# First mixer of an encoder layer: the second pass of its scores over 64 rows, the two banks of a chunk on different halves of TensorE's rows

## The chip, the cores and the metric

One core of one Trainium2 chip runs the whole program. The metric is the device time of one execution in microseconds (us). TensorE (PE) multiplies; its weight loads are told apart as PEld. DVE is the vector engine, ACT the scalar engine, POOL the third elementwise engine, SP issues the DMAs.

## What is computed

One layer on 2048 tokens of width 1024: a normalised input projection, two mixers side by side, an output projection, a squared-ReLU MLP and a gated addition, all in float32. The change concerns the first mixer alone, grouped-query attention with 8 query heads of 64 dimensions on 2 key and value heads:

```python
def block(q_blk):          # 128 queries at a time
    sc = jnp.einsum('bqkgd,bskd->bkgqs', q_blk, k, preferred_element_type=jnp.float32) * scale
    pr = jax.nn.softmax(sc, axis=-1)
    return jnp.einsum('bkgqs,bskd->bqkgd', pr.astype(v.dtype), v)
```

## The kernel before, in words

The program has four phases: the projection, the first mixer (`mixer_a_phase`), the second mixer, and the feed part with output projection, MLP and gate. The first mixer works in 32 units: 16 tiles of 128 queries by 2 key heads, each unit with its group of 4 query heads (G = 4).

**Products in parts.** Matmuls read float32r operands, which hold fewer bits than float32, so an operand is split into a high part (the rounded copy) and a low part (the rest). A head has 64 dimensions and the array 128 rows, so queries and keys are loaded with their 64 dimensions twice. ACT writes the high part of a unit's queries to all 128 rows of `qT` (`query_hi`, L842), and DVE then replaces rows 64 to 127 with the low part (`query_lo`, L897). `kT[g][0]` holds the keys' high part in both halves of the rows, `kT[g][1]` their low part in both. One matmul of `qT` with `kT[g][0]` thus gives high times high plus low times high, and a second pass with `kT[g][1]` adds high times low and low times low.

**Chunks.** A unit's scores are made in 8 chunks (NC), one head by half of the keys. A chunk is 1024 keys, two PSUM banks of 512, and `scores` (L764) issues for each bank the two passes, four matmuls of 128 rows by 512 columns in all, with the same weights. PE's last one increments `sc_done`; DVE takes the negative maximum (`maximum`, L901), ACT the exponential (`exponential`, L848), and the chunk's two banks are free for the chunk after next (`exp_done`).

**The loop.** `pe.Fori(0, NT)` covers two units a turn, and each unit has 16 steps s, one for each 128 keys. In step s PE turns the probabilities of 4 heads (L819, into one of two banks), ACT copies them to `pT[0]` (L876), DVE subtracts for the low part `pT[1]` (L930), and PE multiplies the values of step s - 2 (`values`, L777). In each even step the scores of one chunk of the next unit follow. Step 4 and step 12 also have the sum of the two parts of the output (`fold_out`, L786). Step 6 has the turning of the queries of the unit after next (`turn_queries`, L750); ACT's `query_hi` follows it in its step 7, and so does DVE's `query_lo`. PE's turn of step s waits until DVE has done step s - 2, since it writes the same bank. The order of the work on every engine is written out by hand in these steps; there is no planner. SP's queue brings the queries and stores the results, and POOL does small merges and sums of weight blocks beside it.

**Ahead of the loop** PE turns the queries of units 0 and 1 and all keys, ACT and DVE split them, and the 8 chunks of unit 0 are made. The remaining 256 chunks lie in the loop.

**Outside the mixer** one place matters for what follows: in the projection phase, L372 is a small matmul for bias rows, 33 rows by 8 columns of weights, between full matmuls of L358. It stands directly behind `pe.sem_inc(step, 1)` (L371) and has two records per instruction, since its operands are plain float32. It runs 8 times.

Of the kernel before, what the change touches and what calls it, by code (L numbers as in the profile page):

```python
# [16 lines left out]
F32R = mybir.dt.float32r  # L17
ACT = mybir.ActivationFunctionType
AXX = mybir.AxisListType.X

P = 128
D = 1024
S = 2048
HD = 64
NHA, NKV, NHB = 8, 2, 8
# [11 lines left out]
BANK = 512  # L37
# [512 lines left out]
def mixer_a_phase(nc, scr, ident, fold, heads, w_ff2):  # L550
# [8 lines left out]
    G = NHA // NKV  # L559
    NC = 2 * G  # L560
    NR = 4
    with ExitStack() as ctx:
        k = Kit(nc, ctx, "mixa")
        k_raw = k.sb("k_raw", [P, NT, NKV * 2 * HD])
        v_raw = k.sb("v_raw", [P, NT, NKV * HD])
        kT = [[k.sb(f"kT{g}{h}", [P, S], F32R) for h in range(2)] for g in range(NKV)]
        v_hl = k.sb("v_hl", [P, NT, NKV, 2 * HD], F32R)
        q_in = k.sb("q_in", [P, NHA * 2 * HD])
        qT = [k.sb(f"qT{g}", [P, G, P], F32R) for g in range(NKV)]
        prob = [k.sb(f"prob{u}", [P, G, S]) for u in range(2)]  # L570
        pT = [k.sb(f"pT{h}", [P, NR, BANK], F32R) for h in range(2)]
        oT = k.sb("oT", [P, 2, BANK])
# [11 lines left out]
        score = ctx.enter_context(nc.psum_tensor("mixa_score", [P, 4 * BANK], F32))  # L584
# [157 lines left out]
        @block.tensor  # L742
        def _(pe):
            def turn_queries(V, g, bank, first=False):

                pe.wait_ge(q_dma, (V - g) * 16 + 32)
                if not first:
                    pe.wait_ge(half_done, V * 2 - 2)
                for h in range(G):
                    mm = pe.transpose(bank[:, h * P:(h + 1) * P], q_in[:, (G * g + h) * P:(G * g + h + 1) * P], ident[:])  # L750
                mm.then_inc(qt_done, 1)

            def scores(V, g, c):

                half, h = c // G, c % G
                if c == 0:
                    pe.wait_ge(qt_lo, V + 1)
                if not (isinstance(V, int) and c < 2):
                    pe.wait_ge(exp_done, V * NC + c - 1)
                for j in range(2):  # L760
                    kc = 2 * half + j
                    at = 2 * (c % 2) + j
                    for part in range(2):
                        mm = pe.matmul(score[:, at * BANK:(at + 1) * BANK], qT[g][:, h, :],  # L764
                                       kT[g][part][:, kc * BANK:(kc + 1) * BANK], start=part == 0, stop=part == 1)
                mm.then_inc(sc_done, 1)

            def values(U, g, s):

                half = s // (NT // 2)  # L770
                pe.wait_ge(lo_done, U * NT + s + 3)
                if s == 0:
                    pe.wait_ge(half_done, U * 2 + 1)
                if s == NT // 2:
                    pe.wait_ge(qt_lo, U + 3)
                for part in range(2):
                    mm = pe.matmul(out_acc[half][:], v_hl[:, s, g, :], pT[part][:, s % NR, :],  # L777
                                   start=s % (NT // 2) == 0 and part == 0,
                                   stop=s % (NT // 2) == NT // 2 - 1 and part == 1)
                mm.then_inc(pv_done, 1)  # L780

            def fold_out(count, half):

                pe.wait_ge(o_done, count)
                for h in range(G):
                    mm = pe.matmul(out_acc[half][:, h * HD:(h + 1) * HD], oT[:, half, h * P:(h + 1) * P], fold[:],  # L786
                                   start=True, stop=True)
                mm.then_inc(fold_done, 1)

            pe.wait_ge(q_dma, 32)  # L790
            turn_queries(0, 0, out_acc[0], True)
            turn_queries(1, 1, out_acc[1], True)
            for n in range(2 * NT // 4):
                g, j0 = n % 2, 4 * (n // 2)
                if n % 4 == 0:
                    pe.wait_ge(k_in[n // 4], 32)
                if n >= 6:
                    pe.wait_ge(kt_lo, n - 5)
                for j in range(4):
                    mm = pe.transpose(turn_banks[n % 6][:, j * P:(j + 1) * P], k_raw[:, j0 + j, g * P:(g + 1) * P],  # L800
                                      ident[:])
                mm.then_inc(kt_done, 1)
            pe.wait_ge(kt_lo, 6)
            for c in range(NC):
                scores(0, 0, c)
            pe.wait_ge(kt_lo, 2 * NT // 4)
            pe.wait_ge(v_lo, 1)
            pe.wait_ge(set_done, 4)
            pe.wait_ge(qt_lo, 2)
            pe.matmul(out_acc[1][:], v_hl[:, NT - 3, 1, :], pT[0][:, 2, :], start=True, stop=False)  # L810
            with pe.Fori(0, NT) as it:
                for w in range(2):
                    U = it * 2 + w
                    for s in range(NT):
                        if s in (0, NT // 2):
                            pe.wait_ge(exp_done, U * NC + (G if s == 0 else NC))
                        pe.wait_ge(lo_done, U * NT + s + 1)
                        for h in range(G):
                            mm = pe.transpose(turned[s % 2][:, h * P:(h + 1) * P], prob[w][:, h, s * P:(s + 1) * P],  # L819
                                              ident[:])  # L820
                        mm.then_inc(t_done, 1)
                        if s < 2:
                            values(U - 1, 1 - w, s + NT - 2)
                        else:
                            values(U, w, s - 2)
                        if s % 2 == 0:
                            scores(U + 1, 1 - w, s // 2)
                        if s == 4:
                            fold_out(U * 2 + 1, 1)
                        if s == 6:  # L830
                            turn_queries(U + 2, w, out_acc[1])
                        if s == 12:
                            fold_out(U * 2 + 2, 0)
            values(2 * NT - 1, 1, NT - 2)
            values(2 * NT - 1, 1, NT - 1)
            fold_out(4 * NT + 1, 1)

        @block.scalar
        def _(act):
            def query_hi(V, g, bank):  # L840
                act.wait_ge(qt_done, V + 1)
                act.activation(qT[g][:].rearrange("p h n -> p (h n)"), bank[:], ACT.Copy).then_inc(qt_hi, 1)  # L842

            def exponential(V, par, c):
# [8 lines left out]
            def sums_out(U, half):  # L853

                act.wait_ge(pv_done, U * NT + (half + 1) * NT // 2 + 4)
                act.activation(oT[:, half, :], out_acc[half][:], ACT.Copy).then_inc(o_done, 1)

            query_hi(0, 0, out_acc[0])
            query_hi(1, 1, out_acc[1])
            for n in range(2 * NT // 4):  # L860
                act.wait_ge(kt_done, n + 1)
# [1267 lines left out]
def layer(nc, rel_bias, onehot, x, w_in, rope, ident_d, fold_d, w_ff2, w_tail, g_out, g_mlp_pre, g_ple,  # L2129
          g_attn_pre, g_q, g_k, g_attn_post, g_mlp_post, pT, out):  # L2130

    shapes = {"qA": (S, D_AB), "kA": (S, NKV * 2 * HD), "vA": (S, NKV * HD), "qB": (S, D_AB), "kB": (S, D_AB),
              "vB": (S + 2 * PAD, D_AB), "bias": (NHB, ROWS_W), "table": (NHB, P, ROWS_W),
              "wT": (D_FF // BANK, 5, P, 2 * BANK), "yA": (S + P, D_AB), "yB": (S, D_AB), "h2": (BT, D)}
    scr = {n: nc.dram_tensor(f"scr_{n}", shape, F32, kind="Internal").ap() for n, shape in shapes.items()}

    NF1 = D_FF * D // (P * FeedInputs.CW)
    with nc.semaphore("step") as step, ExitStack() as ctx:
        whole = Kit(nc, ctx, "layer")
        ident, fold = whole.sb("ident", [P, P]), whole.sb("fold", [P, HD])  # L2140
        project_phase(nc, x, w_in, g_attn_pre, g_q, g_k, rope, ident_d, fold_d, rel_bias, onehot, scr, step, ident, fold)
        with ExitStack() as b_ctx:
            heads = HeadInputs(nc, b_ctx, scr)
            mixer_a_phase(nc, scr, ident, fold, heads, w_ff2)
            feed = FeedInputs(nc, ctx)
            mixer_b_phase(nc, scr, step, ident, fold, heads, feed,
                          ((g_out, g_mlp_pre, g_ple), (g_attn_post, g_mlp_post)),
                          [w_tail[NF1 + C] for C in range(FeedInputs.NR4)])
        feed_phase(nc, x, w_ff2, w_tail, pT, scr, out, step, ident, feed)
# [19 lines left out]
```

## Time and profile before

| | us |
|---|---|
| median of 3 runs | 3668.93 |
| lowest and highest | 3666.88, 3674.45 |
| profiled execution, its own time | 3670.11 |
| its span, first to last instruction | 3667.2 |
| mean granted clock of TensorE, of full speed | 0.973 |

| busy | us | share of the span |
|---|---|---|
| PE | 3467.2 | 95% |
| PEld | 2943.7 | 80% |
| DVE | 2394.2 | 65% |
| ACT | 1890.3 | 52% |
| POOL | 1877.0 | 51% |

Busy times are unions of an engine's recorded instructions. Matmuls are pipelined: a matmul's record begins before the one ahead of it has ended, and its end is modelled, so the time that a matmul costs is read from one start to the next. "Idle before" counts only time in which the engine had no record open. "issue" as releaser means that the engine waited for nothing that the profile shows. Times within a timeline are from the span's start.

### The profile page before, as it was taken

To read this page: it belongs to the slowest core of one execution; us is meant where nothing else is said; L and a number is where in the kernel's file an instruction comes from. 1 tells how busy PE (TensorE), PEld (TensorE's weight loads), DVE (VectorE), ACT (ScalarE), POOL (GpSimd) and SP (SyncE) were. 2 spreads that over 40 slices of the span, in tenths; PEclk is the share of its full clock that TensorE was granted. 3 is DMA by queue.
4 is the path that set the end of the run, shared out by engine and by line. 5 is a ranking of instruction groups with operands and counts; after the bars stand their busy time and mean duration, and the time that the engine had idled before them with its cause. 6 is when DMAs were issued, how large, how long until landed. Compare 5 with 4: busy or idle time off the path is not lost.

```text
span 3667.2 us, 56161 instructions
## 1 busy us (share of the span) xinstructions
PE 3467.2 (95%) x18428; PEld 2943.7 (80%) x18428; DVE 2394.2 (65%) x4351; ACT 1890.3 (52%) x3554; POOL 1877.0 (51%) x1188
## 2 busy tenths in 40 slices
PE   7999979999999999999779998999989999899997
PEld 6878768888888889999668887788877888778885
DVE  5434558888888877788465656556565565655554
ACT  2222258888888777778353443334443344433342
POOL 4545512332000034334437777577775777757773
PEclk9999989999999999999889999999999999999998
DMA  4444334443002143344214444345453444434441
GB/s 165 163 170 157 125 105 147 154 154 131 17 17 50 24 91 79 66 90 113 85 63 155 157 145 159 112 151 161 143 162 111 153 160 143 162 109 147 147 151 55
DMA packets 288912, 444.97 MB, mean 121 GB/s; under 512 B 175188, under 2 KB 194076, under 8 KB 282684
## 3 DMA queue, kind: packets, MB, share of 16 engines
q1 hardware_dynamic: 279356, 428.51, 37.4%
q10 hardware_dynamic: 9344, 13.73, 1.0%
q8 instruction: 121, 1.98, 0.2%
q14 instruction: 91, 0.75, 0.1%
HBM read 377.92 MB, written 76.71 MB: 124 GB/s over the span
## 4 chain that ended last, share of the span: by engine, by line
PE 41%; DVE 6%; ACT 2%; issue 1%; POOL 0%; DMA 0%; SPq 0%; DVEq 0%; ACTq 0%
PE feed_bank L1619 41%; DVE feed_res L1927 2%; DVE feed_total L1924 1%; DVE feed_xn L1900 1%; ACT feed_xT L1777 1%; PE feed_bank L1610 1%; DVE feed_xT L1909 0%; POOL feed_w_split L1570 0%; DMA feed_y_in<-scr_yB 0%; DVE feed_ms L1888 0%; DVE feed_total L1984 0%; DVE feed_rec L1891 0%; DVE feed_comb L2011 0%; ACT feed_junk L1752 0%; DVE feed_sums L2030 0%
## 5 line engine op out<-in xcount | busy, mean ns | idle before, releaser
L1570 POOL TENSOR_TENSOR feed_w_split<-feed_w_raw,feed_w_split 128x1024 fp32r<-128x1024 f32 x424 | 1076.9, 2549 | 255.2 <-ACT feed_w_split L1805 235.9
L1619 PE MATMUL feed_bank<-feed_w_split,feed_comb 128*128 128x512 f32 x3648 | 855.1, 395 | 27.9 <-DVE feed_sums L2030 10.4
L1619 PEld LDWEIGHTS feed_bank<-feed_w_split,feed_comb 128*128 128x128 f32 x3648 | 690.8, 190 | 181.2 <-DVE feed_sums L2030 12.9
L1619 PE MATMUL feed_bank<-feed_xT,feed_w_split 128*128 128x512 f32 x3072 | 700.7, 390 | 2.5 <-DVE feed_xT L1909 2.5
L1619 PEld LDWEIGHTS feed_bank<-feed_xT,feed_w_split 128*128 128x128 f32 x3072 | 577.5, 188 | 123.2 <-DVE feed_xT L1909 2.9
L358 PE MATMUL proj_bank<-proj_w_split,proj_xT 128*128 128x512 f32 (+1 forms) x1920 | 407.2, 372 | 19.3 <-ACT proj_st L426 16.1
L358 PEld LDWEIGHTS proj_bank<-proj_w_split,proj_xT 128*128 128x128 f32 x1920 | 335.5, 190 | 86.2 <-ACT proj_st L426 20.6
L1567 POOL TENSOR_SCALAR feed_w_split<-feed_w_raw 128x1024 fp32r<-128x1024 f32 x200 | 228.1, 1140 | 340.3 <-issue 307.7
L930 DVE TENSOR_TENSOR mixa_pT<-mixa_turned,mixa_pT 128x512 fp32r<-128x512 f32 x512 | 348.0, 685 | 81.3 <-ACT mixa_pT L876 77.8
L876 ACT ACTIVATE mixa_pT<-mixa_turned 128x512 fp32r<-128x512 f32 x512 | 306.4, 599 | 150.1 <-PE mixa_turned L819 131.8
L777 PE MATMUL mixa_out_acc<-mixa_pT,mixa_v_hl 128*128 128x512 f32 x1028 | 366.2, 438 | 0.5 <-DVE mixa_pT L930 0.5
L1984 DVE TENSOR_TENSOR feed_total<-feed_total,feed_bank 128x512 f32<-128x512 f32 x352 | 224.5, 682 | 195.7 <-PE feed_bank L1619 192.8
L1820 ACT ACTIVATE feed_rl<-feed_bank 128x512 f32<-128x512 f32 x128 | 76.5, 598 | 523.2 <-PE feed_bank L1619 523.2
L1805 ACT ACTIVATE feed_w_split<-feed_w_raw 128x1024 fp32r<-128x1024 f32 x224 | 236.6, 1065 | 189.1 <-PE feed_bank L1619 185.1
L901 DVE TENSOR_REDUCE mixa_nmax<-mixa_score 128x1 f32<-128x1024 f32 x264 | 322.5, 1223 | 13.5 <-PE mixa_score L764 7.5
L819 PE MATMUL mixa_turned<-layer_ident,mixa_prob 128*128 128x128 f32 x2048 | 308.2, 273 | 0.0
L819 PEld LDWEIGHTS mixa_turned<-layer_ident,mixa_prob 128*128 128x128 f32 x2048 | 253.4, 143 | 56.9 <-issue 0.4
L848 ACT ACTIVATE mixa_prob<-mixa_score,mixa_nmax 128x1024 f32<-128x1024 f32 x263 | 294.1, 1118 | 3.9 <-DVE mixa_nmax L901 3.9
L764 PE MATMUL mixa_score<-mixa_kT,mixa_qT 128*128 128x512 f32 x1056 | 289.2, 396 | 6.9 <-ACT mixa_prob L848 6.2
L1953 DVE TENSOR_TENSOR feed_comb<-feed_rl,feed_comb 128x256 fp32r<-128x256 f32 x128 | 155.0, 1211 | 174.2 <-ACT feed_comb L1824 173.9
L764 PEld LDWEIGHTS mixa_score<-mixa_kT,mixa_qT 128*128 128x128 f32 x1056 | 198.5, 188 | 55.7 <-ACT mixa_prob L848 8.7
L696 POOL TENSOR_TENSOR mixa_below<-mixa_nrow,mixa_nmax 128x8 f32<-128x8 f32 x32 | 6.4, 201 | 439.3 <-DVE mixa_nrow L936 439.3
(191 smaller groups left out, 5155.8 us busy)
## 6 DMA issues: line engine op xcount, KB each, us to landing
feed_w_raw<-w_tail_dram SPq DMA_DIRECT2D x200, 512.0 KB, 3.6
feed_w_raw<-scr_wT SPq DMA_DIRECT2D x160, 512.0 KB, 3.3
proj_w_raw<-w_in_dram SPq DMA_DIRECT2D x39, 1024.0 KB, 4.9
feed_w_raw<-w_ff_dram SPq DMA_DIRECT2D x64, 512.0 KB, 3.5
scr_table<-scr_bias SPq DMA_DIRECT2D x8, 1520.0 KB, 9.0
proj_x_t<-x_dram SPq DMA_DIRECT2D x20, 512.0 KB, 6.3
mixa_q_in<-scr_qA SPq DMA_DIRECT2D x36, 256.0 KB, 3.3
mixb_q_in<-scr_qB SPq DMA_DIRECT2D x18, 512.0 KB, 5.6
```

The costliest lines, as they stand in the source:

```text
L358: mm = pe.matmul(acc[t][:, 0:width], xT[u][a][:, k0 + kk, t * P:(t + 1) * P], w[m][:, kk, :], start=first and kk == 0 and q == 0, stop=las ...
L764: mm = pe.matmul(score[:, at * BANK:(at + 1) * BANK], qT[g][:, h, :], kT[g][part][:, kc * BANK:(kc + 1) * BANK], start=part == 0, stop=par ...
L777: mm = pe.matmul(out_acc[half][:], v_hl[:, s, g, :], pT[part][:, s % NR, :], start=s % (NT // 2) == 0 and part == 0, stop=s % (NT // 2) == ...
L819: mm = pe.transpose(turned[s % 2][:, h * P:(h + 1) * P], prob[w][:, h, s * P:(s + 1) * P], ident[:])
L848: act.activation(prob[par][:, h, half * 2 * BANK:(half + 1) * 2 * BANK], score[:, 2 * (c % 2) * BANK:2 * (c % 2 + 1) * BANK], ACT.Exp, bia ...
L876: act.activation(pT[0][:, s % NR, :], turned[s % 2][:], ACT.Copy).then_inc(hi_done, 1)
L901: ve.tensor_reduce(nmax[:, par, c // G, c % G:c % G + 1], score[:, 2 * (c % 2) * BANK: 2 * (c % 2 + 1) * BANK], AXX, ALU.max, negate=True) ...
L930: ve.tensor_tensor(pT[1][:, s % NR, :], turned[s % 2][:], pT[0][:, s % NR, :].bitcast(F32), ALU.subtract).then_inc(lo_done, 1)
L1567: pool.tensor_scalar(w_sp[0][:, slot, :], w_raw[:, slot, :], 1.0, 0.0, ALU.mult, ALU.add).then_inc(w_hi, 1)
L1570: pool.tensor_tensor(w_sp[1][:, slot, :], w_raw[:, slot, :], w_sp[0][:, slot, :].bitcast(F32), ALU.subtract).then_inc(w_lo, 1)
L1619: mm = pe.matmul(dst, lhs, rhs, start=start, stop=stop)
L1805: act.activation(w_sp[0][:, slot, :], w_raw[:, slot, :], ACT.Copy).then_inc(w_hi_ff, 1)
```

## The change

The scores' first pass stays as it is: two matmuls, one for each bank of the chunk, over 128 rows with `kT[g][0]`. The second pass is now over 64 rows. For the first bank it takes rows 0 to 63 of `qT` (the high part) and of `kT[g][1]`; for the second bank it takes rows 64 to 127 of `kT[g][1]` and of a new buffer `q_hi`, which holds the high part in its upper rows, since there `qT` has the low part. The product of low part by low part is no longer computed. The order of a chunk is now: both banks' first passes, then both second passes, each with its own bank and its own half of the array's rows. ACT writes `q_hi` from the turned queries ahead of its copy to `qT`. The diff:

```diff
@@ mixer_a_phase
         qT = [k.sb(f"qT{g}", [P, G, P], F32R) for g in range(NKV)]
+        q_hi = [k.sb(f"q_hi{g}", [P, G, P], F32R) for g in range(NKV)]
@@ def scores(V, g, c), on PE
                 if not (isinstance(V, int) and c < 2):
                     pe.wait_ge(exp_done, V * NC + c - 1)
+                kc, at = 2 * half, 2 * (c % 2)
                 for j in range(2):
-                    kc = 2 * half + j
-                    at = 2 * (c % 2) + j
-                    for part in range(2):
-                        mm = pe.matmul(score[:, at * BANK:(at + 1) * BANK], qT[g][:, h, :],
-                                       kT[g][part][:, kc * BANK:(kc + 1) * BANK], start=part == 0, stop=part == 1)
+                    pe.matmul(score[:, (at + j) * BANK:(at + j + 1) * BANK], qT[g][:, h, :],
+                              kT[g][0][:, (kc + j) * BANK:(kc + j + 1) * BANK], start=True, stop=False)
+                pe.matmul(score[:, at * BANK:(at + 1) * BANK], qT[g][0:HD, h, :],
+                          kT[g][1][0:HD, kc * BANK:(kc + 1) * BANK], start=False, stop=True)
+                mm = pe.matmul(score[:, (at + 1) * BANK:(at + 2) * BANK], q_hi[g][HD:P, h, :],
+                               kT[g][1][HD:P, (kc + 1) * BANK:(kc + 2) * BANK], start=False, stop=True)
                 mm.then_inc(sc_done, 1)
@@ def query_hi(V, g, bank), on ACT
                 act.wait_ge(qt_done, V + 1)
+                act.activation(q_hi[g][HD:P, :, :].rearrange("p h n -> p (h n)"), bank[HD:P, :], ACT.Copy)
                 act.activation(qT[g][:].rearrange("p h n -> p (h n)"), bank[:], ACT.Copy).then_inc(qt_hi, 1)
```

## Rows read from the trace of the kernel before

**Rows 1.** The page: busy time by engine; busy tenths of PE in 40 slices.

```profile
PE 3467.2 (95%) x18428; PEld 2943.7 (80%) x18428; DVE 2394.2 (65%) x4351; ACT 1890.3 (52%) x3554; POOL 1877.0 (51%) x1188
...
PE   7999979999999999999779998999989999899997
```

**Rows 2.** Busy times by stretch: that of the loop, behind the columns.

```profile
core 0: us, PE busy (x) PEld busy (x) DVE busy (x) ACT busy (x) POOL busy (x), PEclk, DMA share, GB/s
...
507.60:1279.00 771.40, 771.38 (x4739) 658.88 (x4739) 682.35 (x928) 625.38 (x1152) 143.17 (x200) 1.00 0.26 84
```

**Rows 3.** Groups by line of 507 to 1279 us: busy us, mean ns, idle before.

```profile
L777 PE MATMUL mixa_out_acc<-mixa_pT,mixa_v_hl 128*128 128x512 f32 x1026 | 365.4, 438 | 0.0
L930 DVE TENSOR_TENSOR mixa_pT<-mixa_turned,mixa_pT 128x512 fp32r<-128x512 f32 x512 | 348.0, 685 | 81.3 <-ACT mixa_pT L876 77.8
...
L819 PE MATMUL mixa_turned<-layer_ident,mixa_prob 128*128 128x128 f32 x2048 | 308.2, 273 | 0.0
L876 ACT ACTIVATE mixa_pT<-mixa_turned 128x512 fp32r<-128x512 f32 x512 | 306.4, 599 | 150.1 <-PE mixa_turned L819 131.8
...
L764 PE MATMUL mixa_score<-mixa_kT,mixa_qT 128*128 128x512 f32 x1024 | 279.6, 394 | 0.0
...
L786 PE MATMUL mixa_out_acc<-layer_fold,mixa_oT 128*128 128x64 f32 x512 | 63.9, 268 | 0.0
```

**Rows 4.** Timeline of PE, two steps of the loop: start us, us, engine and line, count.

```profile
883.40 1.09 PE L764 MATMUL mixa_score<-mixa_kT,mixa_qT 128*128 128x512 f32 x4
884.33 0.60 PE L819 MATMUL mixa_turned<-layer_ident,mixa_prob 128*128 128x128 f32 x4
...
885.25 0.60 PE L819 MATMUL mixa_turned<-layer_ident,mixa_prob 128*128 128x128 f32 x4
...
886.14 0.40 PE L764 MATMUL mixa_score<-mixa_kT,mixa_qT 128*128 128x512 f32 x1
```

**Rows 5.** Timeline of PE's weight loads in the first of these steps.

```profile
883.41 0.65 PEld L764 LDWEIGHTS mixa_score<-mixa_kT,mixa_qT 128*128 128x128 f32 x3
884.10 0.14 PEld L819 LDWEIGHTS mixa_turned<-layer_ident,mixa_prob 128*128 128x128 f32 x1
```

**Rows 6.** Timelines around the bias matmul L372, first and last place; its line.

```profile
40.47 0.39 PE L358 MATMUL proj_bank<-proj_w_split,proj_xT 128*128 128x512 f32 x1
40.79 0.10 PEld L372 LDWEIGHTS proj_bank<-proj_oh,proj_rb 33*8 33x8 f32 x2 [0.35 <-issue]
...
41.11 0.48 PE L372 MATMUL proj_bank<-proj_oh,proj_rb 33*8 33x380 f32 x1
...
41.52 0.50 PE L358 MATMUL proj_bank<-proj_w_split,proj_xT 128*128 128x512 f32 x1
...
41.52 0.30 PEld L358 LDWEIGHTS proj_bank<-proj_w_split,proj_xT 128*128 128x128 f32 x2 [0.64 <-issue]
...
371.31 0.48 PE L372 MATMUL proj_bank<-proj_oh,proj_rb 33*8 33x380 f32 x1
...
371.72 0.19 PEld L358 LDWEIGHTS proj_bank<-proj_w_split,proj_xT 128*128 128x128 f32 x1 [0.64 <-issue]
...
  issue: 2.8, 8
```

**Rows 7.** Timeline of DVE ahead of the loop: one of the pairs of maxima.

```profile
492.99 2.35 DVE L901 TENSOR_REDUCE mixa_nmax<-mixa_score 128x1 f32<-128x1024 f32 x2 [1.40 <-PE mixa_score L764]
```

**Rows 8.** Timelines of ACT and DVE around a unit's query tile.

```profile
882.73 0.59 ACT L842 ACTIVATE mixa_qT<-mixa_out_acc 128x512 fp32r<-128x512 f32 x1
883.21 0.61 ACT L876 ACTIVATE mixa_pT<-mixa_turned 128x512 fp32r<-128x512 f32 x1
...
883.59 0.69 DVE L897 TENSOR_TENSOR mixa_qT<-mixa_out_acc,mixa_qT 64x512 fp32r<-64x512 f32 x1
884.32 0.69 DVE L930 TENSOR_TENSOR mixa_pT<-mixa_turned,mixa_pT 128x512 fp32r<-128x512 f32 x1
```

**Rows 9.** Timeline of ACT at the mixer's start: first copy for kT.

```profile
482.40 0.60 ACT L862 ACTIVATE mixa_kT<-mixa_turned 128x512 fp32r<-128x512 f32 x1 [1.84 <-PE mixa_turned L800]
```

## The prediction, made before the changed kernel was run

> **What bounds the kernel now.** I began with the page's busy shares and slices [rows 1]: TensorE is the busiest engine of the whole run, and the slices from about 550 to 1280 us (the seventh to the fourteenth) are among its fullest. The busy times by stretch [rows 2] then fix the stage of the change. The first mixer's loop runs from 507.6 to 1279.0 us; in it PE is busy for 771.38 of 771.40 us at clock 1.00, DVE for 682.35, ACT for 625.38. So no wait of another engine ends last here. The groups by line [rows 3] say the same: the score matmuls (L764), the turned probabilities (L819) and the values (L777) have 0.0 us of idle time before them, while ACT waits for PE (L876) and DVE for ACT (L930).
>
> A busy PE is not PE at its peak, so I read prices from starts. One pair of steps of the loop is in [rows 4]: four score matmuls from 883.40, the next line from 884.33, the next scores at 886.14. A pair takes 2.74 us, of which the scores hold 0.93, or 0.23 for each of four. The loads show why a matmul of 512 columns can follow so closely [rows 5]: three loads start within the matmuls ahead, and the next line's load already starts at 884.10, beside the last score matmul. Every weight load here is hidden.
>
> There are 264 chunks of scores: 8 ahead of the loop, and 256 in it (1024 L764 matmuls by 4, [rows 3]). What PE gains or loses on a chunk in the loop goes to the end one for one.
>
> **What the change removes.** A chunk had four full matmuls; it gets two full ones and two of 64 rows each. The products need the same number of columns, so the gain comes only if the two 64-row matmuls run side by side. At best one step of 0.23 us goes per chunk, 256 x 0.23 = 59 us.
>
> **What it adds on PE: two changes of the array's layout per chunk**, full to two halves and back. No 64-row matmul of this form is in the trace. The nearest rows are the bias matmul L372, 33 rows by 8 columns, which takes a part of the array and stands between full ones [rows 6]. The last full matmul starts at 40.47; with a hidden load its successor would start 0.23 later, and its load at once. Instead the L372 load starts at 40.79, that is 0.32 after that matmul: 0.23 of stream and 0.09 of emptying. All eight such places have it (idle 2.8 us before 8 loads, 0.35 each, released by nothing that the profile shows). Going back, the second L372 matmul starts at 41.11, and the full load only at 41.52: 0.41, of which 0.32 is its own stream (40.79 to 41.11), so 0.09 again. The last place of its kind shows the same 0.41 (371.31 to 371.72). Then the load itself is exposed: the full matmul is entered at 41.52 with 0.50 instead of 0.39 us, so 0.11 of waiting for weights. Four of the eight places could show this way back, and they agree; at the other four the load came later for data. A full matmul's record is as long there (0.39) as in the loop (0.40, [rows 4]), so the clock was the same. L372 differs in two ways: it narrows columns too, and a semaphore instruction of PE stands just ahead of it, though none stands behind it, where the 0.09 is the same.
>
> The new chunk, from its first matmul to the stream of what follows: first full matmul 0.23; second, to the load of the first half, 0.32; that load 0.11; the distance d from the first half's stream to the second's; the second's stream and the emptying, 0.23 + 0.09 = 0.32; the next line's load, now exposed, 0.11. That is 1.09 + d against 0.93, a loss of 0.16 + d.
>
> d is the open price. If both halves' loads could go together it is about 0; if two 128-column loads must follow one another it is 0.11, the distance at which exposed loads stand (two loads within 0.30, of 0.19 each [rows 6]); if the halves run one after the other it is 0.23. I take 0.11, since that row shows the same loads, exposed, after the same event, and keep both ends. Per chunk +0.27, and 256 x 0.27 = **69 us**; with d = 0, 41 us; with 0.23, 100 us.
>
> On d the Trainium skill speaks for the cheaper end: TensorE: Matmul & The Clock Gate, Part 3, says that loads overlap running matmuls when their row groups differ, and that the tiles of a pack start about 4 ns apart. By that rule d is near 0 and the sum 0.16 a chunk, 41 us. No row here shows two row groups, and the rows' 0.11 decides for me. TensorEngine Tiling (Array Packing), Key Properties, says that changing the tiling mode, not just the tile, drains TensorE; the trace agrees with it where it can, by the 0.09 on either side of L372, and the rule would cover a change of rows alone.
>
> **The eight chunks ahead of the loop** are paced by a ring: DVE waits for PE's scores (1.40 us before each pair of maxima [rows 7]), and PE for ACT. Of the two chunks of a round, one lies on the ring at least: about 4 x 0.27 = 1 us, at most 2.
>
> **What it adds on ACT: one copy of 64 x 512 per unit**, ahead of the copy into qT, 32 in the loop. The number of columns sets such a copy: I price it as the full one, at its step of 0.48 us (882.73 to 883.21 [rows 8]). ACT then has 20.0 us of work in a unit of 24.1, still below PE. What is queued behind it on ACT: the qT copy, the copy of step 8 (883.21) and an exponential. Behind those waits DVE: its subtraction for q at 883.59 would start about 0.25 later, and the one at 884.32 with it, ending near 885.27 instead of 885.01. PE's turn at 885.25 [rows 4] waits for that one, so without a cover a unit would lose about 0.1 us, 3 us in all. The cover is the chunk between 883.40 and 884.33, which now takes 0.27 longer: nothing. At the start two extra copies (1.2 us) go into an idle stretch of 1.84 us ahead of the first copy for kT [rows 9]: nothing. DMAs, SP's and POOL's queues are not touched; no wait is added. Two buffers of 2 KB a partition cost no time.
>
> **Sum**: 69 + 1 = 70 us. On the profiled execution's 3670.1 that gives 3740; it lay 1.2 above the median of the three runs, so on that median **3739 us**.
>
> **The rivals.** *Faster: emptying belongs to the change of columns, not of rows.* Then loads stay hidden, the halves run together and a chunk gives back 0.23 - d: 31 to 59 us, 3610 to 3638, say 3622. It decides at the point where the first half's load starts: below 0.1 us after the second full matmul's start it holds, at 0.32 not. DVE wouldn't stop it (682 us against some 712 to 740), but the 0.1 us on ACT's copy would then show. For it: L372 changes columns too, and its way in has a semaphore instruction. Against it: the way back has none, and the full-size changes of operand type (scores to L786, [rows 3]) leave no idle time. Chance 0.14. *A cheap switch:* weights exposed but no emptying, 0.18 less per chunk: +0.09 with d = 0.11, or -0.02 with d = 0; 3664 to 3693. Chance 0.10, half of it within the band. *No concurrency:* the halves run one after the other, or the program doesn't place them on different rows. d = 0.23, +0.39 a chunk, 100 + 2 us: 3771. For it: every matmul pair in the trace is at least one stream apart. Chance 0.12. The forecast's own case, with d from 0 to 0.11 (3711 to 3739), has 0.64.
>
> **Numbers.** A measurement of this kernel can tell about 0.2%, 7 us, from no change. Slower: 0.64 + 0.12 + 0.05 = 0.81. Same: 0.05. Faster: 0.14. The range takes in the forecast's bounds, the serial case and the dear half of the cheap switch: 3678 to 3773. That leaves out the rival on the other side and little more.
>
> **What would show it.** In the groups by line, L764 splits into full and 64-row forms, 528 matmuls each, and idle time grows before the loads of L764 and of what follows it. In the timeline the first half's load starts 0.32 after the second full matmul's start, and the scores of a chunk hold 1.20 of a pair of 3.01 us instead of 0.93 of 2.74. The loop stretches by 69 us and no other stage by over 1; DVE and ACT keep their busy times but for 15 to 19 us on ACT. The two 64-row matmuls' starts give d. The prediction is wrong if a hidden load is seen at the entry, if the halves' starts stand 0.23 apart, or if DVE's waits for ACT grow where PE then waits.

## The result: 3713 us against 3672, and the profile after

The changed kernel takes 3713.39 us (median of 4 runs, 3712.64 to 3718.74), the kernel before 3671.69 (4 runs, 3666.88 to 3675.16, three of them those of the table before). The ratio of the two means is 1.0118, with a 95% interval of 1.0100 to 1.0135, which is 37 to 50 us: slower, by 41.7 us from median to median, and clear of noise. The forecast was 3739, within 3678 to 3773. The sign was right and the loss forecast (70 us) 1.7 times what was measured.

The profiled execution took 3718.74 us (span 3716.5). The page's busy times of the changed kernel, which answer to [rows 1]:

```profile
PE 3518.1 (95%) x18428; PEld 2877.6 (77%) x18428; DVE 2398.9 (65%) x4351; ACT 1911.1 (51%) x3588; POOL 1876.7 (50%) x1188
```

PE has 51 us more of busy time, ACT 21 more, and DVE 5. PEld has 66 us *less*, although no load was taken out. Most of that is no time won: the loads of a chunk's two halves stand in the same hundredth (below), so of two groups of 46.9 us each only one counts in the union. The loop's stretch in the changed kernel, from its first turning matmul to its last (behind the columns of [rows 2]):

```profile
515.83:1327.17 811.34, 809.58 (x4735) 586.16 (x4734) 685.89 (x927) 643.82 (x1183) 142.78 (x200) 1.00 0.25 80
```

The same stretch of the kernel before, from 507.91 to 1277.76 us:

```profile
507.91:1277.76 769.85, 769.85 (x4734) 658.01 (x4733) 681.11 (x927) 624.60 (x1151) 143.17 (x200) 1.00 0.26 84
```

The loop grew from 769.85 to 811.34, by 41.5 us, at the same clock of 1.00. Within the noise that is the whole difference of the medians. (The profiled execution was 5 us above its own median, and 6 us of its span lie in the projection, which the change does not touch: its last matmul starts at 469.71 before and 475.71 after, and in another run of the changed scores, below, at 469.89.) Once the loop runs evenly, a unit takes 25.31 us instead of 24.00, read from the turning matmuls' starts.

Groups by line of that stretch, to be held beside [rows 3]. L765 and L767 are the two halves, L822 the turned probabilities, L789 the fold, L880 and L934 ACT's and DVE's parts of them:

```profile
L934 DVE TENSOR_TENSOR mixa_pT<-mixa_turned,mixa_pT 128x512 fp32r<-128x512 f32 x511 | 348.3, 687 | 104.1 <-ACT mixa_pT L880 98.6
L822 PE MATMUL mixa_turned<-layer_ident,mixa_prob 128*128 128x128 f32 x2048 | 319.0, 278 | 1.8
...
L880 ACT ACTIVATE mixa_pT<-mixa_turned 128x512 fp32r<-128x512 f32 x511 | 306.0, 599 | 170.9 <-PE mixa_turned L822 166.7
...
L822 PEld LDWEIGHTS mixa_turned<-layer_ident,mixa_prob 128*128 128x128 f32 x2047 | 237.3, 142 | 85.5 <-issue 31.8 <-DVE mixa_pT L934 23.5
...
L765 PE MATMUL mixa_score<-mixa_kT,mixa_qT 64*128 64x512 f32 x256 | 128.1, 500 | 0.0
...
L789 PEld LDWEIGHTS mixa_out_acc<-layer_fold,mixa_oT 128*128 128x128 f32 x512 | 61.9, 191 | 15.8 <-issue 15.8
...
L767 PEld LDWEIGHTS mixa_score<-mixa_kT,mixa_q_hi 64*128 64x128 f32 x256 | 46.9, 183 | 0.0
L765 PEld LDWEIGHTS mixa_score<-mixa_kT,mixa_qT 64*128 64x128 f32 x256 | 46.9, 183 | 93.4 <-issue 93.4
...
L901 DVE TENSOR_TENSOR mixa_qT<-mixa_out_acc,mixa_qT 64x512 fp32r<-64x512 f32 x32 | 22.3, 696 | 17.2 <-ACT mixa_qT L846 17.2
```

The new idle time stands before the loads: 93.4 us before 256 loads of the first half, 0.36 each, put down to "issue", that is to nothing that the profile shows; 31.8 us before 128 loads of L822, 15.8 before 64 of L789. Nothing stands before L767's loads. The starts show the order. Timelines of PE and of its weight loads in one pair of steps, to be held beside [rows 4, 5]:

```profile
901.39 0.62 PE L763 MATMUL mixa_score<-mixa_kT,mixa_qT 128*128 128x512 f32 x2
901.95 0.50 PE L765 MATMUL mixa_score<-mixa_kT,mixa_qT 64*128 64x512 f32 x1
901.95 0.50 PE L767 MATMUL mixa_score<-mixa_kT,mixa_q_hi 64*128 64x512 f32 x1
902.38 0.66 PE L822 MATMUL mixa_turned<-layer_ident,mixa_prob 128*128 128x128 f32 x4
...
903.34 0.60 PE L822 MATMUL mixa_turned<-layer_ident,mixa_prob 128*128 128x128 f32 x4
...
904.24 0.39 PE L763 MATMUL mixa_score<-mixa_kT,mixa_qT 128*128 128x512 f32 x1
```

```profile
901.16 0.42 PEld L763 LDWEIGHTS mixa_score<-mixa_kT,mixa_qT 128*128 128x128 f32 x2
901.95 0.18 PEld L765 LDWEIGHTS mixa_score<-mixa_kT,mixa_qT 64*128 64x128 f32 x1 [0.36 <-issue]
901.95 0.18 PEld L767 LDWEIGHTS mixa_score<-mixa_kT,mixa_q_hi 64*128 64x128 f32 x1
902.38 0.42 PEld L822 LDWEIGHTS mixa_turned<-layer_ident,mixa_prob 128*128 128x128 f32 x4 [0.24 <-issue]
```

The first half's load starts at 901.95, not beside the matmul ahead of it, as in [rows 5]; the second's stands in the same hundredth, and so do the two matmuls. The next line's load starts 0.43 later.

### The profile page after: what moved, and what is told of

Same layout as the page of the kernel before. It is cut to its first block, busy times and chain, and to the rows that moved or that the text cites. A ratio compares the mean times of both kernels' runs of the same rounds, so it can differ in the third digit from the quotient of the medians.

```text
span 3716.5 us, 56195 instructions
## 1 busy us (share of the span) xinstructions
PE 3518.1 (95%) x18428; PEld 2877.6 (77%) x18428; DVE 2398.9 (65%) x4351; ACT 1911.1 (51%) x3588; POOL 1876.7 (50%) x1188
## 4 chain that ended last, share of the span: by engine, by line
PE 41%; DVE 6%; ACT 2%; issue 1%; POOL 0%; DMA 0%; SPq 0%; DVEq 0%; ACTq 0%
PE feed_bank L1623 40%; DVE feed_res L1931 2%; DVE feed_total L1928 1%; DVE feed_xn L1904 1%; ACT feed_xT L1781 1%; PE feed_bank L1614 1%; DVE feed_xT L1913 0%; POOL feed_w_split L1574 0%; DMA feed_y_in<-scr_yB 0%; DVE feed_ms L1892 0%; DVE feed_total L1988 0%; DVE feed_comb L2015 0%; ACT feed_junk L1756 0%; DVE feed_rec L1895 0%; DVE feed_sums L2034 0%
## 5 line engine op out<-in xcount | busy, mean ns | idle before, releaser
L934 DVE TENSOR_TENSOR mixa_pT<-mixa_turned,mixa_pT 128x512 fp32r<-128x512 f32 x512 | 349.0, 687 | 104.1 <-ACT mixa_pT L880 98.6
L880 ACT ACTIVATE mixa_pT<-mixa_turned 128x512 fp32r<-128x512 f32 x512 | 306.6, 599 | 171.1 <-PE mixa_turned L822 166.9
L822 PE MATMUL mixa_turned<-layer_ident,mixa_prob 128*128 128x128 f32 x2048 | 319.0, 278 | 1.8
L822 PEld LDWEIGHTS mixa_turned<-layer_ident,mixa_prob 128*128 128x128 f32 x2048 | 237.5, 142 | 85.6 <-issue 31.8
L1623 PE MATMUL feed_bank<-feed_w_split,feed_xT 128*128 128x512 f32 x768 | 185.5, 402 | 9.0 <-ACT feed_total L1788 6.6
L316 POOL TENSOR_SCALAR proj_w_split<-proj_w_raw 128x2048 fp32r<-128x2048 f32 x36 | 72.5, 2014 | 219.5 <-ACT proj_st L426 104.5
```

The costliest lines, as they stand in the source:

```text
L880: act.activation(pT[0][:, s % NR, :], turned[s % 2][:], ACT.Copy).then_inc(hi_done, 1)
L934: ve.tensor_tensor(pT[1][:, s % NR, :], turned[s % 2][:], pT[0][:, s % NR, :].bitcast(F32), ALU.subtract).then_inc(lo_done, 1)
L1623: mm = pe.matmul(dst, lhs, rhs, start=start, stop=stop)
```

## Why the starts already tell most of it

Chunk by chunk: the two full matmuls 0.23 apart, 0.33 from the second to the halves, 0.43 from them to the next line, together 0.99. The next line then runs late by its own load: its four turning matmuls hold 0.66 us of record instead of the 0.60 of the next step (903.34), 0.06 more, or, before the fold, about 0.11. So a chunk costs 1.05, or 1.10 where a fold follows (2 of 8), against 0.93. That is 6 x 0.12 + 2 x 0.17 = 1.06 of the 1.31 us per unit. The rest had to be elsewhere, and the profile names a place: DVE's subtraction for the queries (L901) now waits 17.2 us for ACT, 0.54 in each of 32 units. Timelines of ACT, DVE and PE around it, beside [rows 8]:

```profile
910.10 0.60 ACT L880 ACTIVATE mixa_pT<-mixa_turned 128x512 fp32r<-128x512 f32 x1 [0.69 <-PE mixa_turned L822]
910.72 0.59 ACT L845 ACTIVATE mixa_q_hi<-mixa_out_acc 64x512 fp32r<-64x512 f32 x1
911.33 0.60 ACT L846 ACTIVATE mixa_qT<-mixa_out_acc 128x512 fp32r<-128x512 f32 x1
911.82 0.59 ACT L880 ACTIVATE mixa_pT<-mixa_turned 128x512 fp32r<-128x512 f32 x1
```

```profile
911.96 0.69 DVE L901 TENSOR_TENSOR mixa_qT<-mixa_out_acc,mixa_qT 64x512 fp32r<-64x512 f32 x1 [0.54 <-ACT mixa_qT L846]
912.68 0.69 DVE L934 TENSOR_TENSOR mixa_pT<-mixa_turned,mixa_pT 128x512 fp32r<-128x512 f32 x1
```

```profile
912.25 0.66 PE L822 MATMUL mixa_turned<-layer_ident,mixa_prob 128*128 128x128 f32 x4
...
913.43 0.66 PE L822 MATMUL mixa_turned<-layer_ident,mixa_prob 128*128 128x128 f32 x4
```

PE's turn of step 9 starts at 912.25 and that of step 10 at 913.43, 1.18 apart, while two such steps, the first behind a chunk, stand 0.96 apart where PE isn't held (902.38 to 903.34 above). The missing 0.22 ends when DVE's subtraction of 912.68 does (913.37).

**My theory** was then: about 1.08 us of a unit are two layout changes per chunk, 0.22 are this stall, nothing else. **Rivals**: the layout changes alone make up the 1.31; the halves only seem to run together; what costs is the new order of the banks and not the layout; a price that comes once per chunk and not per change.

## The experiments

Ten kernels ran. In the table, "before" is the kernel before on the same chip (medians of 3673.6 beside e1 to e4, 3672.3 beside e5 to e7, 3673.7 beside e8 to e10), and a ratio stands with its 95% interval.

| run | us | ratio to before | unit, us |
|---|---|---|---|
| changed kernel | 3713.4 | 1.0118 (1.0100 to 1.0135) | 25.31 |
| e1_copy_split | 3705.7 | 1.0088 (1.0075 to 1.0102) | 25.07 |
| e2_same_half | 3768.5 | 1.0250 (1.0234 to 1.0265) | 26.87 |
| e3_order_only | 3671.8 | 0.9997 (0.9988 to 1.0006) | 24.00 |
| e4_copy_only | 3682.2 | 1.0022 (1.0012 to 1.0033) | 24.38 |
| e5_alternate | 3869.7 | 1.0536 (1.0512 to 1.0560) | 29.96 |
| e6_halves_first | 3723.3 | 1.0138 (1.0120 to 1.0157) | 25.57 |
| e7_pairs | 3877.7 | 1.0555 (1.0536 to 1.0573) | 30.14 |
| e8_half_max | 3670.0 | 0.9993 (0.9982 to 1.0003) | 24.00 |
| e9_pairs_half_max | 3789.3 | 1.0312 (1.0289 to 1.0335) | 27.63 |
| e10_pairs_early | 3839.3 | 1.0454 (1.0429 to 1.0478) | 29.04 |

### e1: the stall on ACT taken away

```diff
 def query_hi(V, g, bank):        # ACT
-    act.activation(q_hi[g][HD:P, ...], bank[HD:P, :], ACT.Copy)
-    act.activation(qT[g][:], bank[:], ACT.Copy).then_inc(qt_hi, 1)
+    act.activation(q_hi[g][HD:P, ...], bank[HD:P, :], ACT.Copy).then_inc(qt_hi, 1)
+    act.activation(qT[g][0:HD, ...], bank[0:HD, :], ACT.Copy).then_inc(qt_low, 1)
 def query_lo(V, g, bank):        # DVE
-    ve.tensor_tensor(lower, bank[HD:P, :], lower, ALU.subtract)
+    ve.tensor_tensor(lower, bank[HD:P, :], upper, ALU.subtract)   # upper = q_hi[g][HD:P]
```

PE waits for `qt_low` as well wherever it waits for `qt_lo`.

> The changed kernel, but ACT's two copies for the queries are in another order and of 64 partitions each: first the high part into the upper rows of q_hi, which at once releases DVE's subtraction (it now subtracts q_hi), then the high part into rows 0 to 63 of qT, behind it. The work on PE is the same. Theory: of the 1.31 us that a unit got longer (24.00 to 25.31), 1.08 are PE's layout changes and 0.22 a stall of PE's turn of step 10, which waits for DVE, which waited 0.54 for ACT's second copy. So a unit takes 25.09, 7 us less in all, 3706, and DVE's 17 us of waiting for qT are gone. Rival: the layout changes alone make up the 1.31; then the unit stays at 25.31 and the time at 3713.

Measured 3705.74, unit 25.07. DVE in this run, the same place in a unit:

```profile
901.22 0.69 DVE L906 TENSOR_TENSOR mixa_qT<-mixa_out_acc,mixa_q_hi 64x512 fp32r<-64x512 f32 x1
```

The query subtraction (L906) follows the one ahead of it without a wait. The 0.24 per unit is the stall, 32 x 0.24 = 7.7 us, and 1.07 per unit is left on PE. The times alone would not tell 7 us apart here, since the intervals of the two ratios overlap; the units and the vanished wait do. The rival that gives the layout changes all of the 1.31 falls.

### e4: the same stall, made in the kernel before

```diff
 def query_hi(V, g, bank):        # kernel before; nobody reads q_hi
     act.wait_ge(qt_done, V + 1)
+    act.activation(q_hi[g][HD:P, ...], bank[HD:P, :], ACT.Copy)
     act.activation(qT[g][:], bank[:], ACT.Copy).then_inc(qt_hi, 1)
```

> The kernel before, with the extra ACT copy into q_hi ahead of the copy into qT, and nobody reads q_hi. PE's work is that of before. Theory: ACT takes 0.60 us longer to the query tile, DVE's subtraction and the one behind it start 0.37 later, and PE's turn of step 10 waits about 0.19 a unit: 32 x 0.19 = 6 us, 3676. Rival (the prediction's words): 0.1 a unit without a cover, 3 us; or nothing.

Measured 3682.23, 8 us slower by the ratio (its interval is 4 to 12 us), and 24.38 per unit: 0.38 and not 0.19, or 12 us over 32 units. The size was missed here as in the prediction, by the same step, the price of the copy. ACT and PE of this run:

```profile
890.37 0.60 ACT L878 ACTIVATE mixa_pT<-mixa_turned 128x512 fp32r<-128x512 f32 x1 [0.57 <-PE mixa_turned L820]
890.99 0.59 ACT L843 ACTIVATE mixa_q_hi<-mixa_out_acc 64x512 fp32r<-64x512 f32 x1
891.59 0.60 ACT L844 ACTIVATE mixa_qT<-mixa_out_acc 128x512 fp32r<-128x512 f32 x1
892.09 0.59 ACT L878 ACTIVATE mixa_pT<-mixa_turned 128x512 fp32r<-128x512 f32 x1
```

```profile
893.70 0.66 PE L820 MATMUL mixa_turned<-layer_ident,mixa_prob 128*128 128x128 f32 x4 [0.17 <-DVE mixa_pT L932]
```

ACT's copy for step 7 starts at 890.37 and that for step 8 at 892.09: 1.72 apart with the extra copy. In the kernel before the same two stand 0.97 apart (858.22 and 859.19 in the trace). One copy thus costs 0.75, not the 0.48 that the prediction had taken from two full copies in a row, nor the 0.60 of this run's expectation: the copy of 64 partitions starts only when the record ahead of it has ended (890.99), and the full one again (891.59). It isn't the height alone that does this: in e1 the copy into rows 0 to 63 also starts 0.62 after the one into rows 64 to 127, but the full copy behind it follows 0.49 later (901.11 to 901.60), as behind a full one. In these rows the late starts are those where the first row changes between 0 and 64; no run varied that alone. Besides, PE's held turn (893.70, idle 0.17 for DVE) pays its load in the open: its record is 0.66 for four instead of 0.60. From ACT's copy for step 7 to PE's turn of step 10 it is 3.33 us here (890.37 to 893.70) and 3.33 in the changed kernel (910.10 to 913.43): the path over ACT and DVE is equally long in both, and only what PE has to do meanwhile differs. That is why the same copy costs 0.38 a unit here and 0.24 there.

### e3: the order of the banks alone

```diff
-                for j in range(2):
-                    ...
-                    for part in range(2):
+                for part in range(2):
+                    for j in range(2):
+                        ...
```

> The kernel before, but a chunk's four full matmuls in the changed order: both banks' first passes, then both second passes. No 64-row matmul. Theory (the layout changes cost): as before, 3669 to 3672, a chunk still 0.93 us. Rival (going back to a bank that was left, or ending on both banks at once, costs or delays DVE's maximum): slower by up to the 35 us that I put down to layout changes.

Measured 3671.83 against 3673.58, unit 24.00. Leaving a bank and coming back to it costs nothing that these runs can tell (the interval ends 2 us above the kernel before): that rival falls.

### e2: both halves on the same rows

```diff
-                mm = pe.matmul(score[..bank 1..], q_hi[g][HD:P, h, :], kT[g][1][HD:P, ..bank 1..], ...)
+                mm = pe.matmul(score[..bank 1..], qT[g][0:HD, h, :], kT[g][1][0:HD, ..bank 1..], ...)
```

> The changed kernel, but both second-pass matmuls take rows 0 to 63 (qT's high part, the keys' low part in its lower rows); q_hi and its copy are gone. Same products, same two layout changes per chunk, but no two halves side by side. Theory: the two 64-row matmuls, now 0.003 us apart, come to stand 0.23 apart, 256 x 0.23 = 59 us and 1 to 2 ahead of the loop; the stall of 7 us by ACT's second copy goes. 3713 + 59 + 1 - 7 = 3766. Rival: the halves do not really run at the same time, and the records only show them so; then the time without the stall is 3706.

Measured 3768.45. PE in this run:

```profile
900.38 0.50 PE L764 MATMUL mixa_score<-mixa_kT,mixa_qT 64*128 64x512 f32 x1
900.72 0.39 PE L766 MATMUL mixa_score<-mixa_kT,mixa_qT 64*128 64x512 f32 x1
901.04 0.66 PE L821 MATMUL mixa_turned<-layer_ident,mixa_prob 128*128 128x128 f32 x4
```

The halves start 0.34 apart, 0.11 of it the first one's exposed load, and the next line follows 0.32 later: 0.66 from the first half to the next line, against 0.43 in the changed kernel. The unit grew from the 25.07 of e1, which has no stall either, to 26.87, by 1.80, or 0.23 per chunk. So in the changed kernel the halves do run side by side and save a whole step of 0.23; it is still not enough.

### e5: twice as many layout changes

```diff
-                (both full passes, then both halves)
+                for j in range(2):
+                    (full pass of bank j, then its 64-row pass on its own rows)
```

> The changed kernel, but bank by bank: full pass of bank 0, its 64-row pass on rows 0 to 63, full pass of bank 1, its 64-row pass on rows 64 to 127. Four layout changes per chunk and never two halves together. Theory, each change at its measured price: first full to first half 0.327, half to the next full 0.430, that one's exposed load 0.108 and on to the second half 0.327, to the next line 0.430, and 0.056 for its load: 1.68 against 0.93, +0.75 a chunk, 192 us in the loop, with the stall 7 and a few ahead of the loop: 3872 (3865 to 3880). Rival (most of a change's cost comes once per chunk, as waiting for the bank or for the semaphore): about 3713 + 59 = 3772 to 3800.

Measured 3869.67. PE in this run, one chunk:

```profile
900.32 0.40 PE L764 MATMUL mixa_score<-mixa_kT,mixa_qT 128*128 128x512 f32 x1
900.65 0.49 PE L766 MATMUL mixa_score<-mixa_kT,mixa_qT 64*128 64x512 f32 x1
901.07 0.50 PE L764 MATMUL mixa_score<-mixa_kT,mixa_qT 128*128 128x512 f32 x1
901.50 0.50 PE L766 MATMUL mixa_score<-mixa_kT,mixa_q_hi 64*128 64x512 f32 x1
901.93 0.55 PE L821 MATMUL mixa_turned<-layer_ident,mixa_prob 128*128 128x128 f32 x3
```

0.33, 0.42, 0.43 and 0.43 from start to start: each change costs its price wherever it stands. A unit grew by 5.96, or 0.745 per chunk, against the 0.75 that four changes were to cost. The price is per change, not once per chunk. The stall, which the expectation had added, isn't in it: PE's turns of steps 9 and 10 stand 0.96 apart, as where PE isn't held.

```profile
898.46 0.66 PE L821 MATMUL mixa_turned<-layer_ident,mixa_prob 128*128 128x128 f32 x4
...
899.42 0.60 PE L821 MATMUL mixa_turned<-layer_ident,mixa_prob 128*128 128x128 f32 x4
```

The chunk ahead of them has become so long that it covers the extra copy.

### e6: what an exit costs hangs on what follows

An exit is the change from the halves back to the full array.

```diff
-                (both full passes with start=True, then both halves with stop=True)
+                (both halves with start=True, then both full passes with stop=True)
```

> The changed kernel with the 64-row pass of a chunk ahead of the full one, so the halves follow the values' matmuls and the full scores stand behind the halves. Same number of layout changes. Theory: what an exit costs hangs on the load that it exposes; a full load for matrix products has records of 0.19, one for the turning of probabilities 0.14, and the latter follows 6 of a unit's 8 chunks in the changed kernel. Now a load of 0.19 follows each: +0.05 for 6 chunks, 0.3 a unit, 10 us; 3723. Rival: an exit costs the same whatever follows, 3713.

Measured 3723.33, unit 25.57 against 25.31 in the changed kernel. As with e1, it is the unit and the starts that show the 10 us; the intervals of the two ratios overlap. PE in this run:

```profile
901.28 0.73 PE L767 MATMUL mixa_score<-mixa_kT,mixa_qT 128*128 128x512 f32 x2
901.86 0.60 PE L822 MATMUL mixa_turned<-layer_ident,mixa_prob 128*128 128x128 f32 x4
```

The two full matmuls now stand 0.34 apart (901.28 with 0.73 for two, next line 901.86) instead of 0.23: behind the exit, the first pays 0.11 for its load. Before a turning matmul it was 0.06. Groups by line have the records: 188 ns for a load of products, 142 for one of L822.

### e7 to e10: fewer visits to the halves

Call a visit the way from the full array to the halves and back. If a visit costs about 0.36 and each pair of halves gives 0.23 back, two chunks on one visit should win. What could stand against it is the ring of the four score banks: PE fills them, DVE takes the maxima, ACT the exponentials, and only then are they free for PE again. e7 makes the scores of two chunks at every fourth step:

```diff
-                        if s % 2 == 0:
-                            scores(U + 1, 1 - w, s // 2)
+                        if s % 4 == 0:
+                            scores(U + 1, 1 - w, s // 2)     # chunks c and c + 1: 4 full, then 2 x 2 halves
```

DVE's maxima follow in steps s % 4 = 0 and 1, ACT's exponentials in steps 1 and 3.

> Two chunks per visit to the halves, on top of the split copy: at every fourth step PE makes the full passes of two chunks and then their four 64-row matmuls (two pairs), so a unit has 4 visits instead of 8. DVE's and ACT's work is moved by a step, and the scores of the next pair need both banks of the last pair back. Theory on PE alone: a visit costs about 0.36 and a pair of halves saves 0.23, so two chunks on one visit would win 0.10 over the kernel before, 13 us in all. But the ring of four banks (maxima 2.4 us, exponentials 2.4 us, turns between them) is longer than the 3.65 us that PE leaves it: PE waits some 0.8 us per visit for ACT's exponential, 100 us; 3740 to 3800, and the profile shows PE idle for ACT mixa_prob. Rival (the ring holds): 3660.

Measured 3877.67: slower, as expected, but by much more than the range, and not for the reason given. The waits of its loop:

```profile
ACT mixa_pT L886 <- PE mixa_turned L826: 324.8, 192, 3.3
DVE mixa_pT L939 <- ACT mixa_pT L886: 231.8, 256, 2.4
...
PEld mixa_turned L826 <- DVE mixa_pT L939: 170.8, 190, 1.4
...
PEld mixa_score L764 <- ACT mixa_prob L858: 32.3, 64, 0.9
```

PE waits little for ACT's exponential (32.3 us before the loads of the scores). It waits for DVE's subtractions of the turned probabilities (170.8 us before loads), DVE for ACT's copies (231.8), and ACT for PE's turns (324.8). e8 and e9 shorten DVE's maxima, the control without and the test with pairs; e9 and e10 move an exponential forward and let each chunk wait for its own banks alone.

```diff
-  score[:, 2 * (c % 2) * BANK:2 * (c % 2 + 1) * BANK]        # the maximum's input
+  score[:, 2 * (c % 2) * BANK:2 * (c % 2) * BANK + BANK]     # e8, e9
-                        if s % 4 in (1, 3):                  # e7's second exponential
+                        if s % 4 in (1, 2):                  # e9, e10
```

> Leaves work out: the kernel before, but DVE takes each maximum over the first 512 of a chunk's 1024 scores, so the softmax's shift is another. A control for the next run. PE sets the loop's time, DVE only gets 0.5 us shorter per chunk: unit 24.0, time as before, 3672.

> Leaves out the same work (maxima over half of the scores), with two chunks per visit to the halves: 4 visits a unit. The scores of a chunk wait only for their own two banks, and the second exponential stands one step earlier than in the kernel of pairs. Theory: with the shorter maxima the ring of banks takes about 3.3 to 3.8 us beside the 3.65 that PE leaves it, so PE mostly sets the pace, and a pair of chunks costs 1.73 us instead of 1.86: unit 23.5 to 23.8, 3657 to 3667. Rival (a visit costs more with two chunks on it, or pairs stall in another place too): 3690 or more.

> The kernel of the run before this one, with the full maxima again; nothing left out. Theory: the ring (two maxima 2.4, the second exponential 1.3, a turn's subtraction 0.65 between them) is 4.4 us or more beside 3.65 to 4.1, so PE waits 0.4 to 1 us on each of 4 visits: unit 25.5 to 28, 3720 to 3800, less than the 3878 of the kernel of pairs, in which the exponentials also held up ACT's copies. Rival: the ring is no bound, and it comes out as the run before.

e8 came out as the kernel before: DVE is no bound there. e9 missed its range by 122 us and e10 by 39. PE in e9, one visit:

```profile
904.55 1.07 PE L764 MATMUL mixa_score<-mixa_kT,mixa_qT 128*128 128x512 f32 x4
905.55 0.49 PE L768 MATMUL mixa_score<-mixa_kT,mixa_qT 64*128 64x512 f32 x1
...
905.89 0.39 PE L768 MATMUL mixa_score<-mixa_kT,mixa_qT 64*128 64x512 f32 x1
...
906.21 0.66 PE L826 MATMUL mixa_turned<-layer_ident,mixa_prob 128*128 128x128 f32 x4
```

PE's own price is what I had worked out: 904.55 to 906.21 is 1.66 for two chunks, 1.72 with the exposed load (1.77 on the half of the visits that a fold follows), against 1.86. But the loop took 883.92 us. Its groups:

```profile
L939 DVE TENSOR_TENSOR mixa_pT<-mixa_turned,mixa_pT 128x512 fp32r<-128x512 f32 x510 | 348.6, 689 | 318.2 <-ACT mixa_pT L886 318.2
...
L886 ACT ACTIVATE mixa_pT<-mixa_turned 128x512 fp32r<-128x512 f32 x511 | 305.3, 604 | 265.9 <-PE mixa_turned L826 265.9
...
L826 PEld LDWEIGHTS mixa_turned<-layer_ident,mixa_prob 128*128 128x128 f32 x2048 | 232.4, 142 | 175.9 <-DVE mixa_pT L939 130.5 <-issue 23.4
...
L751 PEld LDWEIGHTS mixa_out_acc<-layer_ident,mixa_q_in 128*128 128x128 f32 x128 | 13.4, 140 | 45.0 <-DVE mixa_y_half L917 45.0
```

The stall is not the ring of the score banks: PE's score matmuls (L764) have 0.0 us of idle time before them in e9. PE makes no turn of probabilities during a visit, so ACT and DVE, which were busy for 625 and 681 of the 770 us before, idle for a visit (ACT 265.9 us before its copies, DVE 318.2), and afterwards both maxima and both exponentials stand between the copies for which PE's turns wait (130.5 us before L826's loads). That the visit's length starves them is my reading of these rows; no run varied it alone. There is a second place beside it: PE's turning of the queries (L751) waits for DVE's output of the unit before (L917), 45.0 us before its loads, where the kernel before has 4.2 and no engine that they wait for; no run tried why that output comes late. And e10, which differs from e9 by the full maxima alone, takes 50 us more, though no idle time stands before its score matmuls either: in the kernels of pairs DVE's time lies on the path, in the kernel before it doesn't (e8). No version that beats the kernel before came out, and what holds up the kernels of pairs stays open.

## Why the prediction was right, and where its sum was off

**What bounds the loop, and that PE's loss goes through one for one:** held. The loop grew by 41.5 us, the runs by 41.7, DVE and ACT still wait. It held of PE's own work; the 7 to 8 us of the copy, below, are a wait of PE for another engine, which the prediction had named as a sign that it was wrong: DVE's subtraction for the queries waits 17.2 us for ACT, and PE for DVE behind it.

**The price of a layout change from L372** [rows 6]: held, and this decided the sign. Emptying was 0.09 there on either side; in the changed kernel the half's load starts 0.33 after the full matmul's start (forecast 0.32), and the next line's 0.43 after the halves (0.11 + 0.32). That L372 narrows columns too, and that a semaphore instruction stands ahead of it, did not matter: a change of rows alone costs the same. The rival "faster" needed a hidden first load, and the "cheap switch" one at the end of the stream, 0.23 after the second full matmul's start; it stands at 0.33, and all 256 first loads have idle time before them, 0.36 in the mean.

**d, the distance of the halves:** this step of the sum failed. "I take 0.11, since that row shows the same loads, exposed, after the same event." It measured 0.00 (the starts of L765 and L767, and of their loads, stand in the same hundredth). The row had two loads for the same rows, one behind the other. The sum with d = 0, which the prediction kept as its cheap end, was 41 us. TensorE: Matmul & The Clock Gate, Part 3, in the Trainium skill had spoken for that end: the tiles of a pack start about 4 ns apart. The trace agrees with it, with 3 ns between the starts of the two halves. The serial rival is out by e2. Of the 35 us between the forecast for the loop (69 us) and what PE's own work lost (34), 28 are this step: 256 x 0.11.

**The exit's load:** priced at 0.11 for every chunk, it is 0.06 before the turning matmuls (6 of 8 chunks). With both corrections a chunk loses 0.13 in the mean, 34 us in the loop (1.07 x 32). The scores' pair of steps takes 2.85 us (901.39 to 904.24) instead of 2.74; the forecast was 3.01.

**ACT's extra copy: "nothing".** Wrong, 7 to 8 us (e1). Both parts of the step failed: the copy took 0.75 of ACT's time and not 0.48, and the chunk named as its cover grew by 0.11 to 0.12 and not by 0.27, so it hid less. ACT's busy time grew by 21 us, where 15 to 19 were forecast. The error ran against that of d and of the load, so it is luck that the result stands on the cheap end (41 us): 34 + 8 = 42. The sign, and that the time fell within the range, rest on the price of the layout change and are no luck.

**Ahead of the loop:** 1 to 2 us were expected. From the first turned query (477.99, 483.85) to the loop's start (507.91, 515.83) it is 29.92 before and 31.98 after, 2.1 us. But it is 30.4 in e1, and 29.8 in e4 and 30.2 in e3, whose score matmuls are full: single profiles can't tell whether it is 0 or 2.

## What to carry to other kernels

A half-height matmul pays only if a visit to the other layout carries more than it costs: here a visit cost 0.35 to 0.40 us (0.09 to empty the array on either side, 0.11 and 0.06 to 0.11 for loads that had been hidden) and gave back one step of 0.23. Look in the old trace for any odd-shaped matmul between full ones: the gaps at its two sides price a layout change before anything is built. And an extra copy on an engine with 19% of idle time isn't free if it stands on the chain for which a turn of PE waits; release the waiting engine by the first of two copies, as in e1.

## What the runs showed of the hardware

- Two matmuls of 64 x 512 on different halves of the rows start 0.00 us apart, and so do their loads; on the same rows 0.34, of which 0.11 is the first one's exposed load (e2).
- A change between the full array and its halves holds the next load until about 0.09 us after the last stream, both ways (0.33 and 0.43 from start to load).
- An exposed load costs 0.11 us ahead of matrix products (e6) and 0.06 ahead of turning matmuls (0.66 for four instead of 0.60).
- An ACT copy of 64 x 512 between two full ones took 0.75 us from the chain, where full copies in a row stand 0.48 to 0.49 apart (e4).
